# Prompt value products of a chunk-causal attention step: from full fp32 to three fp32r passes over split operands

## The reference, cut to what matters

```python
logits = jnp.einsum('bqgrd,bqkgd->bqgrk', qg, k_sel) * ATTN_SCALE
logits = jnp.where(valid[:, :, None, None, :], logits, -jnp.inf)
p = jax.nn.softmax(logits, axis=-1)
o = jnp.einsum('bqgrk,bqkgd->bqgrd', p.astype(v_sel.dtype), v_sel)
```

## Time and profile before

| | |
|---|---|
| median of the timed runs | 1322.52 us |
| the profiled execution's own time | 1326.4 us |
| its span, first to last instruction | 1324.6 us |
| PE busy | 1258.0 us (95%) |
| DVE busy | 936.7 us (71%) |
| ACT busy | 501.0 us (38%) |
| POOL busy | 463.2 us (35%) |
| mean granted PE clock | 0.987 |

### The profile page before, as it was taken

The page is one execution under the profiler, slowest core; times in us unless marked ns, Lnnn a source line. Parts: engine busy times, 40 slices in busy tenths (PEclk is TensorE's granted clock), DMA queues, the critical chain, the costliest instruction groups (busy, mean ns, idle before and its releaser), DMA issues.

```text
span 1324.6 us, 21407 instructions
## 1 busy us (share of the span) xinstructions
PE 1258.0 (95%) x7551; PEld 1097.8 (83%) x7551; DVE 936.7 (71%) x2249; ACT 501.0 (38%) x1090; POOL 463.2 (35%) x752
## 2 busy tenths in 40 slices
PE   5999999999989999998999998999999979998996
PEld 5999999999989999998777766999788858776752
DVE  5665888888999998864677766243566568776647
ACT  5554222121212112324665554000423247655644
POOL 4700585869783214654000000220011143333320
PEclk9999999999999999999999999999999989999999
DMA  7201142131212321103000221945320258999849
GB/s 261 72 25 45 60 104 73 44 82 36 72 37 103 100 86 51 33 1 100 1 1 17 68 67 34 319 137 175 120 80 33 96 211 302 345 350 336 317 161 393
DMA packets 79313, 163.85 MB, mean 124 GB/s; under 512 B 12401, under 2 KB 47937, under 8 KB 78065
## 3 DMA queue, kind: packets, MB, share of 16 engines
q1 hardware_dynamic: 64977, 128.84, 28.7%
q0 software_dynamic: 12656, 27.62, 6.3%
q10 hardware_dynamic: 1584, 6.10, 1.1%
HBM read 137.86 MB, written 39.21 MB: 134 GB/s over the span
## 4 chain that ended last, share of the span: by engine, by line
PE 78%; DMA 7%; POOL 5%; DVE 4%; ACT 3%; SPq 2%; issue 2%; POOLq 0%; ACTq 0%; DVEq 0%
PE bank L884 11%; PE bank L883 11%; PE bank L885 11%; PE bank L1093 4%; PE bank L1168 3%; PE bank L1287 3%; PE bank L1162 3%; PE bank L1011 2%; PE bank L1075 2%; PE bank L1179 2%; PE bank L1180 2%; PE bank L1181 2%; DMA region_w<-in_wd 2%; DMA region_q<-in_wd 2%; PE bank L1164 2%; DMA region_q<-expert_rows_scratch 2%
## 5 line engine op out<-in xcount | busy, mean ns | idle before, releaser
L1893 DVE MAX8 small<-region_kv 128x8 f32<-128x272 f32 (+4 forms) x241 | 190.2, 828 | 47.6 <-DVE region_kv L1898 47.5
L883 PE MATMUL bank<-h_hi,w_hi 128*128 128x384 f32 (+1 forms) x576 | 196.1, 340 | 0.0
L884 PE MATMUL bank<-h_lo,w_hi 128*128 128x384 f32 (+1 forms) x576 | 196.0, 340 | 0.0
L1898 DVE MATCH_REPLACE8 region_kv<-small,region_kv 128x272 f32<-128x272 f32 (+4 forms) x241 | 195.5, 818 | 0.0
L885 PE MATMUL bank<-h_hi,w_lo 128*128 128x384 f32 (+1 forms) x576 | 194.4, 338 | 0.0
L2246 POOL TENSOR_TENSOR w_lo<-w_stage,w_hi 128x512 fp32r<-128x512 f32 x64 | 80.8, 1295 | 144.7 <-ACT w_hi L1390 144.6
L883 PE MATMUL bank<-w_hi,h_hi 128*128 128x256 f32 x448 | 128.8, 288 | 2.3 <-ACT region_q L1453 2.3
L885 PE MATMUL bank<-w_hi,h_lo 128*128 128x256 f32 x448 | 125.9, 281 | 0.0
L884 PE MATMUL bank<-w_lo,h_hi 128*128 128x256 f32 x448 | 125.8, 281 | 0.0
L885 PEld LDWEIGHTS bank<-h_hi,w_lo 128*128 128x128 f32 x576 | 108.7, 189 | 0.0
L884 PEld LDWEIGHTS bank<-h_lo,w_hi 128*128 128x128 f32 x576 | 108.2, 188 | 0.6
(11 more groups left out here) (345 smaller groups left out, 3156.7 us busy)
## 6 DMA issues: line engine op xcount, KB each, us to landing
w_stage<-in_w_in SPq DMA_DIRECT2D x72, 256.0 KB, 3.3
region_kv<-in_xa SPq DMA_DIRECT2D x16, 512.0 KB, 6.0
region_q<-in_wg SPq DMA_DIRECT2D x12, 512.0 KB
region_q<-in_wu SPq DMA_DIRECT2D x12, 512.0 KB
region_q<-in_wd SPq DMA_DIRECT2D x12, 512.0 KB
region_w<-in_wg SPq DMA_DIRECT2D x10, 512.0 KB
region_w<-in_wu SPq DMA_DIRECT2D x10, 512.0 KB
region_w<-in_wd SPq DMA_DIRECT2D x10, 512.0 KB
```

What stands on the lines that cost most here:

```text
L883: mm(out, st_hi(k), mv_hi(k), start=(k == 0), stop=False)
L884: mm(out, st_hi(k), mv_lo(k), start=False, stop=False)
L1893: nc.vector.max(m8[:, q, :], x).then_inc(dve_c, 1)
L1898: nc.vector.match_replace(x, m8[:, q, :], x, TAKEN).then_inc(dve_c, 1)
```

## The change

The prompt's value products become three fp32r passes. For that:

- The values are split once into `v_hi` (ACT, three casts of 128x768) and `v_lo` (DVE, three subtractions) during the last query projection.
- ACT's copies of the transposed tiles now write fp32r (`PT_hi`, `PTC_hi`), and DVE subtracts these from the bank (`probs_rest`, new semaphore `a_tl`) to make `PT_lo` and `PTC_lo`. A bank is free for the next transposes only after both.
- DVE's logit chunks are issued in the order of PE's tiles (`ttr_part`), and the rest of tile j follows the chunks of tile j.
- Heads 0 to 2 of every prompt group but the first are scaled by POOL (a power of -1, then the multiplication); head 3 stays on DVE, after the last tile's rest.
- The masks are packed as bf16, which frees the place for `v_hi`. The sample caches have two slots instead of three. The first `wao` block lies in the place of old probabilities, is loaded after step 9 and split in steps 12 (ACT) and 13 (POOL). `w_out` is loaded a little later.

```diff
 def p_trans(x, j):                                   # PE
     if t >= 2:
         pe.wait_ge(a_te, t - 1)
+        pe.wait_ge(a_tl, rests_to(t - 2))
...
 def p_values(x, j):                                  # PE
-    mm(out[:, :], values[0:rows, :], PT[0:rows, t % 3, :], start=(j == 0), stop=False, ...)
+    mm(out, hi, p_hi, start=(j == 0), stop=False, skip_group_check=True)
+    mm(out, lo, p_hi, start=False, stop=False, skip_group_check=True)
+    pe.wait_ge(a_tl, rests_to(t))
+    last = mm(out, hi, p_lo, start=False, stop=(j == nb - 1), skip_group_check=True)
...
 def s_trans(x, part):                                # PE
+    pe.wait_ge(a_tl, rests_to(t - 2))    # part 0;  part 1: rests_to(t - 1)
...
 for st in STEPS[1:]:                                 # PE
-    if st >= 0:
-        pe.wait_ge(a_p, U_AT[PG[st]] + REP)
+    pe.wait_ge(a_p, BY_DVE.index((PG[st], REP - 1)) + 1)
+    if st >= 1:
+        pe.wait_ge(a_pp, (REP - 1) * st)
...
+def probs_rest(x, j):                                # DVE
+    dve.wait_ge(a_te, t + 1)
...
+        tt(PT_lo[0:rows, t % 3, :], bank[3 + t % 2][0:rows, :], PT_hi[0:rows, t % 3, :].bitcast(F32),
+           ALU.subtract).then_inc(a_tl, 1)
...
-nc.vector.memset(PTC[CHUNK:P, :, :], 0.0).then_inc(zero_ready, 1)      # DVE, before step 0
+for part in (PTC_hi, PTC_lo):
+    nc.vector.memset(part[CHUNK:P, :, :].bitcast(F32), 0.0).then_inc(zero_ready, 1)
+for p0, p1 in ((32, 64), (64, P)):
+    nc.vector.memset(PTS_last[p0:p1, :], 0.0).then_inc(zero_ready, 1)
...
 for st in STEPS[1:]:                                 # DVE
+    nb, during, after = plan(st)
+    for j in range(nb):
+        for r, m in during[j]:
+            ttr_part(PG[st + 1], r, m)
+        if j == 0 and st - 1 in S_STEP:
+            scale(S_STEP[st - 1], 0)
+        probs_rest(PG[st], j)
     if st + 1 < NPG:
-        for r in range(REP):
-            ttr(PG[st + 1], r)
-            if r >= 1:
-                scale(PG[st + 1], r - 1)
-            elif st - 1 in S_STEP:
-                scale(S_STEP[st - 1], 0)
         scale(PG[st + 1], REP - 1)
     if st < NPG - 2:
         q_rest(PG[st + 2])
     if st >= 0:
         oevac(PG[st])
...
+def scale(x, r):                                     # POOL
+    pool.wait_ge(a_exp, U_AT[x] + r + 1)
+    link(tt(stat(x, r, "inv"), stat(x, r, "sum"), minus_one, ALU.pow))
+    p = probs_of(x, r)[:, 0:chunks_of(x)[-1][1]]
+    nc.gpsimd.tensor_scalar(p, p, stat(x, r, "inv"), None, ALU.mult).then_inc(a_pp, 1)
+for st in STEPS[1:]:
+    if st - 6 in range(NSB, DEC_B):
+        new_keys(st - 6)
+    if st == 13:
+        wao_lower(0)
+    if st + 1 < NPG:
+        for r in range(REP - 1):
+            scale(PG[st + 1], r)
```

More of the change, by code:

```diff
@@ L514, in build, with rests_to @@
         O_AT = {x: n for n, x in enumerate(PO)}
+        OF_PROMPT = [x[0] == "p" for x in PO for _ in range(trs_of(x))]
+        def rests_to(t):
+            return sum(OF_PROMPT[:t + 1])
+        BY_POOL = [(x, r) for x in PG[1:] for r in range(REP - 1)]
+        BY_DVE = [(PG[0], r) for r in range(REP)]
+        for st in STEPS[1:]:
+            BY_DVE += ([(S_STEP[st - 1], 0)] if st - 1 in S_STEP else []) + ([(PG[st + 1], REP - 1)] if st + 1 < NPG else [])
+        assert len(BY_POOL) + len(BY_DVE) == REP * NPG + DEC_B
         KEY_CHUNKS = splits(SAMPLE0)
@@ L776, in _ @@
             sp.wait_ge(pj_done, NU)
-            for b in range(3):
+            for b in range(NSB):
                 cache_in(b)
@@ L782, in load_wao @@
                     sp.wait_ge(b6_done, 3 * (c - 2))
-                sp.dma_start(wao_raw[c % 3], a["w_ao"][c].rearrange("p (k n) -> p k n", k=KD)).then_inc(wao_in[c % 3], 16)
+                src = a["w_ao"][c].rearrange("p (k n) -> p k n", k=2 if c == 0 else KD)
+                sp.dma_start(wao(c)[0], src).then_inc(wao_in[c % 3], 16)
             def load_x2(t):
@@ L790, in load_gates @@
                 sp.dma_start(sB[:, c % 2, :], sB_d[c, :, :]).then_inc(sbi_in[c % 2], 16)
-            sp.wait_ge(a_sm, S_AT[PG[6]])
+            for b in range(NSB, 5):
+                cache_in(b)
+            sp.wait_ge(a_t, T_AT[PG[9]] + trs_of(PG[9]))
             load_wao(0)
-            for b in range(3, DEC_B):
+            for b in range(5, DEC_B):
                 cache_in(b)
@@ L1603, in first_group_steps @@
                         cp(k_hi_first[m][:, :], kT[:, 0, c0:c1]).then_inc(qk_high, 1)
+                if i == 30:
+                    act.wait_ge(selected, NT)
+                    for q in range(3):
+                        cp(v_hi[:, 3 * q:3 * q + 3, :], vS[:, 3 * q:3 * q + 3, :]).then_inc(v_high, 1)
                 if i in (33, 34, 36, 37):
@@ L1944, in ttr @@
                 ts(stat(x, r, "neg"), src, -ATTN_SCALE, None, ALU.mult).then_inc(a_max, 1)
+            def ttr(x, r):
+                for m in range(len(chunks_of(x))):
+                    ttr_part(x, r, m)
+            def probs_rest(x, j):
+                t = T_AT[x] + j
+                dve.wait_ge(a_te, t + 1)
+                if j == trs_of(x) - 1:
+                    late = bank[3 + t % 2][0:CHUNK, :].rearrange("p (r t) -> p r t", r=REP)[:, :, CHUNK:P]
+                    tt(PTC_lo[0:CHUNK, :, :], late, PTC_hi[0:CHUNK, :, :].bitcast(F32), ALU.subtract).then_inc(a_tl, 1)
+                else:
+                    rows = key_tile(x, j)[1]
+                    tt(PT_lo[0:rows, t % 3, :], bank[3 + t % 2][0:rows, :], PT_hi[0:rows, t % 3, :].bitcast(F32),
+                       ALU.subtract).then_inc(a_tl, 1)
             def scale(x, r):
```

165 lines of the change are left out of this document (106 added, 59 removed).

## The result

| | median of the runs, us | runs | profiled execution: own time, span |
|---|---|---|---|
| before | 1323.19 (1321.86 to 1324.12) | 4 | 1326.4, 1324.6 |
| after | 1334.01 (1332.63 to 1334.16) | 4 | 1334.01, 1332.2 |

The change makes the kernel slower, by less than one per cent: ratio 1.0072, 95% interval 1.0059 to 1.0084. The four executions of before in this table lie low (their medians' quotient would be 1.0082): 62 more of them, beside the experiments, go from 1322.2 to 1327.3 with a median of 1324.4, and 1334.01 over that is 1.0072. So the change costs 9.6 us. The two profiled executions differ by 7.6, because that of before lay 2.0 above 1324.4 and that of after on its own median.

The account below looks back on a forecast made before the run. PE was taken to bound the kernel. Step 0 -0.1, steps 1 to 6 +3.85, 7 to 9 +2.5, 10 to 15 -0.4 sum to +5.8 us, forecast 1328.3 from the median; own range 1323 to 1334, chance 0.52.

Parts of the forecast that it names:

- The saving: Attention value products as three fp32r passes: 0.16 us less per full tile, 0.07 per last tile, 12.6 in all.
- The wait for the subtraction: Attention steps: PE's next transposes wait for DVE's subtraction, queued behind logit chunks; step 2 stalls 0.2, 0.71 and 0.73 us.
- U: Start of a step's first transposes; step 2's first chunk was put at U+1.87, its third transposes' bank at U+4.09.
- the middle stall: Step 2, transposes behind the next tile without logit chunks: subtraction seen after 1.86 us, bank wanted after 1.14; stall 0.73.
- Steps 1 to 6: Attention steps 1 to 6: stalls exceed the saving in each, from +0.29 to +0.96 us, together +3.85.
- my sum of stalls: All new PE stalls of the attention stage added up: 18.4 us.
- Steps 7 to 9: Steps with a sample stream: the first subtraction follows the sample's multiplication; +0.85, +1.04 and +0.6 us, together +2.5.
- rival C: POOL's lock: late GpSimd scaling blocks DVE's head 3 scaling, 1.2 us in 12 steps; +14, 1342; chance 0.1.
- Steps 10 to 15: Saving and new stalls fall into PE's existing wait for ACT: -0.4 to +0.5 us each, -0.4 in sum.
- rival D: PE's clock falls: stalls halve it in four steps, half of 6.5 us each on top of the forecast; 1341; chance 0.03.
- A: Stalls hidden, DVE's queue ahead of PE: full saving gives 1309.9 us, half the stalls 1319.1; chance 0.2.
- B: Saving and stalls cancel, with two thirds of the forecast stalls: 1322.2 us; chance 0.12.

Follow-up runs that it names:

- experiment 1: Kernel after without DVE's 88 subtractions, low part zeroed once, all three value passes kept: 1315.3 us, ratio 0.9936.
- experiment 9: experiment 7's kernel with DVE's subtraction between the first tile's two chunks and ahead of the last chunk tile's chunks: 1327.7 us, ratio 1.0023.
- experiment 8: Kernel after with GpSimd's multiplications left out, reciprocals kept: whole time 1356.2 us, not usable; steps 1 to 6 take 87.22.
- Experiment 5: Kernel after, steps 7 to 15: sample's exponential behind ACT's first copy, its scaling behind DVE's second subtraction: 1330.5 us, ratio 1.0044.
- 7: Kernel after with the orders of experiments 4, 5 and 6 together: 1329.3 us, ratio 1.0026.
- 12: 11's kernel, each order only in steps it had shortened (subtraction ahead 1 to 8, third head on ACT 2, 4, 5): 1322.6 us, ratio 0.9985.
- 11: experiment 9's kernel with the output's rounded copy on ACT, plus ACT scaling the third head in steps 1 to 6: 1327.4 us, ratio 1.0021.
- experiment 3: Kernel after with all four heads scaled by DVE again, none by GpSimd: 1383.1 us, ratio 1.0444.
- experiment 4: Kernel after with ACT's cast of the first output-projection weights moved from head to end of step 12: 1334.4 us, ratio 1.0075.
- 6: Kernel after, steps 1 to 6: next queries' cast and subtraction moved earlier, last head's exponential one copy later: 1333.7 us, ratio 1.0069.

## Why the prediction came out as it did

Forecast 1328.3, or +5.8; measured 1334.0, or +9.6 against before's median of 1324.4 (+7.6 between the profiles). The direction and the mechanism came as forecast, the size was short. Of the 5.7 us that the forecast is low, 1.9 lie in its base: it was added to 1322.5, the median of three executions that lay low.

**The saving held as PE's price, not as time.** Three passes and transposes 1.14 us, as predicted. That the saving is real when nobody waits for the subtraction, experiment 1 shows: 0.9936, some 8.5 to 9 us of the 12.6 in my sum. The rest went into other waits, GpSimd's in step 4 among them.

**The wait for the subtraction held, where it was worked out from rows.** For step 2, from U = 660.79: DVE's first chunk predicted U+1.87, measured U+1.79; third transposes predicted U+4.09, measured U+4.09; the middle stall predicted 0.73, measured 1.96 - 1.14 = 0.82 (669.66 to 671.62); the step predicted +0.45, measured +0.49. Steps 1 to 6 were predicted +3.85 and came to +3.91. PE's rows name the subtraction (17.0 and 1.9 us of waits for it). Experiment 1 shows from one side that it is this wait (without subtractions 18.7 us less), and 9 from the other: the same instructions in another order, and steps 1 to 6 lose 3.9 us. That 18.7 is so near to my sum of stalls, 18.4, is partly luck: experiment 1 also relieves DVE, gets less than the full saving, and ran without the fall in step 12.

**Steps 7 to 9 were undersized:** +2.5 predicted, +3.6 measured. In step 7 the third transposes came at U+4.13. The sample's multiplication ran at U+2.88; I had taken U+2.42 from before's step 8 as if DVE's queue there stayed as it was. But DVE now starts such a step later too: by 0.1 in experiment 8, where it runs at U+2.53, and by 0.35 more in the kernel after, because DVE's multiplication ahead of it is held up beside GpSimd's. I had moved one queue and not what stands in it, and left rival C's price out of the sum. Experiment 5 shows how much of it is order alone: 1.5 us of the 3.6.

**Steps 10 to 15 were missed, step 12 above all, for the clock.** The prediction has them between -0.4 and +0.5 each, -0.4 in sum; steps 10 to 14 came to +1.39. Step 11 has +0.70, step 12 +1.62. Without the fall step 12 has +0.29 (11.57 in experiment 8 against 11.28), within my bounds. What I left out is small: of the moved cast I only asked whether the weights would be ready in time, not what is queued behind it on ACT, the first copy of turned probabilities, and that is 0.4. The fall is 1.3.

**So rival D came true once, in small.** I gave it 0.03 and thought of four steps; it fell once in the stage, for 3.5 us, and I had taken the pocket of the earlier trace rows (1.34 of 3.00 us busy without a fall) as proof that short waits are harmless. Of the 12 experiments nine have a fall, most of them at other places; 5, 7 and 12 have none. Each count is of one execution.

**The whole difference** of 9.6 is 2.0 more than that of the profiles, which is what before's profiled execution has above 1324.4. About 1.5 of it is the fall at 830 in that execution. The 3.8 between +5.8 and +9.6 are then 1.1 in steps 7 to 9, 1.8 in steps 10 to 14 (1.3 of it the clock's), and 0.9 outside these steps, which stays open. How often such falls come in the executions without a profile stays open.

**Rival C was rightly given little, but its mechanism is there.** I feared DVE's multiplication beside a running GpSimd. In the kernel before, where GpSimd does not multiply, and in experiment 8 DVE's multiplication of a given width takes the same time each time, to 0.01. Beside one of GpSimd's it takes 0.90 in place of 0.56 in the kernel after (729.15) and 0.71 in place of 0.43 (771.68), and ends 0.2 to 0.4 behind GpSimd's. That cost step 7 its 0.35. It doesn't happen each time: in experiment 9 it runs from 699.03 to 699.66 inside GpSimd's (698.21 to 700.46) and takes its usual 0.63. What decides is not shown. By the Trainium skill, "SBUF — State Buffer", section "Who interferes with whom", one of the two would be blocked for the whole of the other if DVE were in its two-port mode. The trace agrees for some pairs and not for others, and no row tells DVE's mode. What was right in C is also the margin: GpSimd is the next bound as soon as the waits are gone (experiments 9 and 11).

**A and B** asked that DVE's queue be ahead of PE. With another order (12) it nearly is, and the result is B's: both cancel, ratio 0.9985. The full saving, A, was seen in no kernel that does the subtraction.

## What to carry to other kernels

A cheaper product on the bounding engine is worth its saving only if the extra operand is made by an engine whose queue reaches it in time; what counts is the place in the queue, not the engine's share of busy time (DVE had 13% of step 2 free, and PE waited for it twice there). Before moving an instruction to cover, write down what is queued behind it on that engine and who waits for that, through all engines: a copy on ACT that stood alone before is now the first link of a chain over ACT, DVE and PE. Compare with a base of many executions: three of them put this one 1.9 us too low, a third of the forecast difference. And try an order step by step: the same order took 3.9 us off steps 1 to 6 and put 1.1 on steps 10 to 13.

## What the runs showed of the hardware

- TensorE's granted clock fell from 1.00 to 0.5 (2.4 to 1.2 GHz) for some 3.5 us at a time, after stretches in which PE waited for 0.4 to 1.8 us, most often several times; in experiment 3, with waits of up to 4.1 us, it stayed down for 6 to 13 us. In experiment 4 it fell at 769 after four microseconds with 0.56, 0.57, 0.76 and 0.61 us busy; before's pocket of 1.34 in 3.00 us did not make it fall. Falls of 3.5 us made their step 1.3 to 1.6 us longer (steps 9 to 13 of the kernel after and of experiments 4, 6, 9 and 11).
- GpSimd's multiplication by a scalar took 2.57 us for 128x912 and 2.25 for 128x784, DVE's 0.69 and 0.63; GpSimd's power of one column took 0.57, DVE's reciprocal 0.15.
- DVE's multiplication of fp32 in SBUF by a scalar can be held up beside GpSimd's: 0.95 in place of 0.63 us (784 columns), 0.90 in place of 0.56 (656), 0.94 in place of 0.49 (528) in the kernel after and in experiment 9; other pairs ran side by side at their usual times (0.63 inside 2.25 at 699.03 in experiment 9).
- GpSimd can be the one that is held up. In step 12 of the kernel after its 128x272 multiplication took 1.49 us in place of 0.97, beginning at 809.33, 0.02 us after DVE's subtraction of two SBUF operands, which took its usual 0.67. In experiment 9 the same subtraction ran inside GpSimd's multiplication (696.95, 0.68 us, inside 695.33 to 697.58), and both took their usual time.
